# Two blocks of transformer in one kernel: the modulation vectors' pieces move from VectorE to ScalarE and GpSimd

## The reference

```
x = first_block(x, ...)         # 2 layers: dilated attention + FFN, gated linear attention + FFN
# second_block: 2 layers, each with N_MOD = 9 modulation vectors of D = 1024
c_act = silu(c)                                         # (1, 1024)
mod = split(c_act @ w_ada[l] + b_ada[l], 9)             # w_ada[l]: 1024 x 9216
h = modulate(rms_norm_2(x, ffn1_norm[l]), mod[0], mod[1])
...
def swiglu(h, w_gate_up, w_down):
    g, u = split(h @ w_gate_up, 2)
    return (silu(g) * u) @ w_down
```

## Time and profile before

| | |
|---|---|
| time, median of 3 runs | 3469.39 us (3467.5 to 3470.66) |
| profiled execution: its time and its span | 3467.5 us and 3467.5 us |
| busy: PE, PEld (weight loads) | 3438.4 us (99%), 2906.9 us (84%) |
| busy: DVE, ACT, POOL | 2446.7 us (71%), 1515.5 us (44%), 187.7 us (5%) |
| chain of work that ended last, by engine | PE 94%, DVE 3%, issue 1%, ACT 1% |
| DMA | 444.89 MB, mean 128 GB/s |

### The profile page before, as it was taken

How to read it: one execution, slowest core, us unless ns; L and a number is a source line. 1 busy time by engine, 2 the same in 40 slices (tenths; PEclk the granted TensorE clock), 3 DMA queues, 4 the chain that set the end, 5 groups by cost and what they waited for, 6 DMA issues and landing times.

```text
span 3467.5 us, 51118 instructions
## 1 busy us (share of the span) xinstructions
PE 3438.4 (99%) x19728; PEld 2906.9 (84%) x19728; DVE 2446.7 (71%) x4223; ACT 1515.5 (44%) x2603; POOL 187.7 (5%) x266
## 2 busy tenths in 40 slices
PE   9999999999999999999999999999999999999999
PEld 7777777888876788888999888899989998878998
DVE  5777775777766577777667767766686667677666
ACT  5555554322343332234444444444454444444444
POOL 0000000000000000000110000010001100000100
PEclk9999999999999999999999999999999999999999
DMA  4222223667421267744655322465446543225654
GB/s 148 80 73 77 80 65 104 223 220 227 129 72 55 73 223 219 226 156 116 152 143 144 86 73 79 128 150 145 126 133 152 147 122 89 68 69 154 152 145 108
DMA packets 207827, 444.89 MB, mean 128 GB/s; under 512 B 28976, under 2 KB 78512, under 8 KB 207600
## 3 DMA queue, kind: packets, MB, share of 16 engines
q1 hardware_dynamic: 171952, 325.55, 30.5%
q0 software_dynamic: 35648, 116.28, 14.2%
HBM read 438.73 MB, written 2.10 MB: 127 GB/s over the span
## 4 chain that ended last, share of the span: by engine, by line
PE 94%; DVE 3%; issue 1%; ACT 1%; DMA 0%; SPq 0%; DVEq 0%; ACTq 0%
PE psP L1423 18%; PE psP L1428 18%; PE psP L1424 18%; PE psS L1572 7%; PE psS L1573 7%; PE psS L1571 7%; PE psP L1653 3%; PE psP L1660 3%; PE psP L1654 3%; PE psS L1996 1%; PE psS L1716 1%; PE psM L2019 1%; PE psS L1880 1%; PE psS L1685 1%; PE psS L1698 0%
## 5 line engine op out<-in xcount | busy, mean ns | idle before, releaser
L1423 PE MATMUL psP<-a_hi,w_hi 128*128 128x512 f32 x1736 | 686.7, 396 | 1.2 <-ACT a_hi L1376 1.2
L1428 PE MATMUL psP<-a_lo,w_hi 128*128 128x512 f32 x1736 | 677.6, 392 | 0.0
L1424 PE MATMUL psP<-a_hi,w_lo 128*128 128x512 f32 x1736 | 676.8, 390 | 0.0
L819 ACT ACTIVATE w_hi<-raw 128x1024 fp32r<-128x1024 f32 (+3 forms) x411 | 341.4, 831 | 398.5 <-PE psP L1428 398.5
L2112 DVE TENSOR_TENSOR w_lo<-raw,w_hi 128x1024 fp32r<-128x1024 f32 (+3 forms) x411 | 386.7, 941 | 164.0 <-ACT w_hi L819 160.7
L1423 PE MATMUL psP<-h_hi,w_hi 128*128 128x512 f32 x1024 | 407.2, 398 | 4.1 <-ACT h_hi L911 2.3
L1424 PE MATMUL psP<-h_hi,w_lo 128*128 128x512 f32 x1024 | 399.4, 390 | 0.0
L1423 PEld LDWEIGHTS psP<-a_hi,w_hi 128*128 128x128 f32 x1736 | 326.8, 188 | 79.2 <-issue 15.8
L1428 PE MATMUL psP<-h_lo,w_hi 128*128 128x512 f32 x1024 | 391.8, 391 | 0.0
L2503 DVE TENSOR_TENSOR s_lo<-s_raw,s_hi 128x1024 fp32r<-128x1024 f32 (+1 forms) x288 | 314.5, 1092 | 104.8 <-ACT s_hi L982 104.7
L1428 PEld LDWEIGHTS psP<-a_lo,w_hi 128*128 128x128 f32 x1736 | 325.7, 188 | 71.2 <-DVE a_lo L3169 0.9
(11 more groups left out here) (412 smaller groups left out, 6146.8 us busy)
## 6 DMA issues: line engine op xcount, KB each, us to landing
s_raw<-in_gu SPq DMA_DIRECT2D x360, 256.0 KB, 3.5
adaw<-in_ada POOLq DMA_DIRECT2D x96, 768.0 KB, 5.4
raw<-in_gu SPq DMA_DIRECT2D x120, 512.0 KB, 3.7
s_raw<-in_gu POOLq DMA_DIRECT2D x144, 256.0 KB, 4.1
raw<-in_down SPq DMA_DIRECT2D x128, 256.0 KB, 2.9
raw<-in_qkv SPq DMA_DIRECT2D x40, 512.0 KB, 3.5
raw<-in_mix_in SPq DMA_DIRECT2D x34, 512.0 KB, 3.5
raw<-in_qkv SPq DMA_DIRECT2D x64, 256.0 KB, 3.0
```

What stands on the lines that cost most here:

```text
L819: nc.scalar.activation(w_hi[:, s, 0:cols], raw[:, s, 0:cols], copy).then_inc(hi_done, 1)
L1423: nc.tensor.matmul(psP[:, s, :], hi, rhs[0](kt), start=(n == 0), stop=False)
L1424: nc.tensor.matmul(psP[:, s, :], lo, rhs[0](kt), start=False, stop=False)
L1428: mm = nc.tensor.matmul(psP[:, s, :], w_hi[:, s, kt * P:kt * P + P], rhs[1](kt), start=False, stop=(n == K - 1))
```

## The change

A piece is now treated by two engines. ScalarE multiplies it by its column of cact: for kt = 0 into ada_acc, and for kt = 1 to 7 in place, in adaw. GpSimd then adds adaw to ada_acc, seven additions in each group. The slots are the same 60, now on ScalarE (ada_scale), always right behind hi. VectorE keeps only the folding, in the tenth slot of a group where it had the ninth. GpSimd issues the load of piece c + 4 behind the addition of piece c (for kt = 0, behind its scaling).

```
@@ GpSimd
+            def ada_load(c):
+                if c >= ADA_RING:
+                    old = c - ADA_RING
+                    if old % KT == 0:
+                        pool.wait_ge(ada_scaled, old + 1)
+                    else:
+                        pool.wait_ge(*ada_added.at(added_before(old) + 1))
+                pool.dma_start(adaw[:, c % ADA_RING, :], A["ada"][c]).then_inc(ada_landed[c % ADA_RING], 16)
+            def ada_add(c):
+                group, kt = divmod(c, KT)
+                pool.wait_ge(ada_scaled, c + 1)
+                if kt:
+                    total = ada_acc[:, group % 2, :]
+                    pool.wait_ge(*ada_added.at(added_before(c)))
+                    nc.gpsimd.tensor_tensor(total, total, adaw[:, c % ADA_RING, :], ALU.add).then_inc(ada_added.sem, 1)
             for F in (F0, F1):
                 pool.wait_ge(F.norm.acc_ready, F.norm.turns(0) + 1)
-                for c in range(F.ada * 48, F.ada * 48 + 48):
-                    pool.wait_ge(ada_used, c + 1)
-                    pool.dma_start(adaw[:, c % ADA_RING, :], A["ada"][c]).then_inc(ada_landed[c % ADA_RING], 16)
+                first_piece = F.ada * 48
+                for c in range(first_piece, first_piece + ADA_RING):
+                    ada_load(c)
+                for c in range(first_piece, first_piece + 48):
+                    ada_add(c)
+                    if c + ADA_RING < first_piece + 48:
+                        ada_load(c + ADA_RING)
@@ ScalarE, ffn
+                def ada_scale(count):
+                    for _ in range(count):
+                        group, kt = next(slices)
+                        if kt >= KT:
+                            continue
+                        c = group * KT + kt
+                        w, to = adaw[:, c % ADA_RING, :], ada_acc[:, group % 2, :]
+                        act.wait_ge(ada_landed[c % ADA_RING], (c // ADA_RING + 1) * 16)
+                        if kt == 0 and group >= 2:
+                            act.wait_ge(ada_folded, group - 1)
+                        nc.scalar.activation(w if kt else to, w, copy, scale=cact[:, kt:kt + 1]).then_inc(ada_scaled, 1)
                         hi(3, shapes[2 * j + 3])
+                        ada_scale(1)
                         pos.step()
...
                         hi(3, shapes[2 * j + 4])
+                        ada_scale(ADA_PER_PAIR - 1)
                         pos.step()
...
                         hi(3, shapes[2 * nf + m + 3])
+                        if not last:
+                            ada_scale(ADA_PER_DOWN)
                         pos.step()
@@ VectorE, folded
-                dve.wait_ge(ada_used, ADA_RING + (g + 1) * KT)
+                dve.wait_ge(*ada_added.at((g + 1) * (KT - 1)))
@@ VectorE, ffn
-                    dve.wait_ge(ada_landed[c % ADA_RING], (c // ADA_RING + 1) * 16)
-                    dve.wait_ge(ada_used, c + ADA_RING)
-                    if kt == 0:
-                        i = v.tensor_scalar(total, w, at, None, ALU.mult)
-                    else:
-                        i = v.scalar_tensor_tensor(total, w, at, total, ALU.mult, ALU.add)
-                    i.then_inc(ada_used, 1)
...
-                        if kt < KT:
-                            ada(group * KT + kt)
-                        elif kt == KT:
+                        if kt == KT + 1:
                             folded(group)
```

More of the change, by code:

```diff
@@ L528, in program @@
         cact_ready = sem("cact_ready")
-        ada_used = sem("ada_used")
+        ada_scaled = sem("ada_scaled")
         ada_folded = sem("ada_folded")
@@ L565, in program @@
         root_copied, ffn_silu, ffn_high = (Later(z, TOKEN_TILES - 8) for z in (probT1_ready, hlog_ready, hrstd_ready))
+        ada_added = Later(rot_ready, TOKEN_TILES - 8)
         ffn_rooted, r_silu = Later(hvar_ready, TOKEN_TILES - 8), Later(exp1_done, TOKEN_TILES - 8)
@@ L784, in _, with added_before @@
                 pool.dma_start(xT[:, p, :], A["x"][:, p, :]).then_inc(x_back[p], 16)
+            def added_before(c):
+                return c - c // KT - 1
+            def ada_load(c):
[13 more added lines that the diff above has]
+                    nc.gpsimd.tensor_tensor(total, total, adaw[:, c % ADA_RING, :], ALU.add).then_inc(ada_added.sem, 1)
             for F in (F0, F1):
                 pool.wait_ge(F.norm.acc_ready, F.norm.turns(0) + 1)
-                for c in range(F.ada * 48, F.ada * 48 + 48):
-                    pool.wait_ge(ada_used, c + 1)
-                    pool.dma_start(adaw[:, c % ADA_RING, :], A["ada"][c]).then_inc(ada_landed[c % ADA_RING], 16)
+                first_piece = F.ada * 48
[5 more added lines that the diff above has]
+                        ada_load(c + ADA_RING)
             def weight_sums(F, l):
@@ L921, in ffn @@
                 root_copy(F.norm, ffn_root)
+                first_group = 2 * len(PARTS) * F.ada
+                slices = iter([(group, kt) for group in range(first_group, first_group + 2 * len(PARTS)) for kt in range(KT + 2)])
+                def ada_scale(count):
[9 more added lines that the diff above has]
+                        nc.scalar.activation(w if kt else to, w, copy, scale=cact[:, kt:kt + 1]).then_inc(ada_scaled, 1)
                 for n, (f0, nf) in enumerate(PARTS):
@@ L945, in ffn @@
                             stream_square(m, N)
+                assert next(slices, None) is None
                 if g:
@@ L2353, in ffn @@
             def ffn(F, N, g, after_first):
-                def ada(c):
-                    group, kt = divmod(c, KT)
-                    w, total, at = adaw[:, c % ADA_RING, :], ada_acc[:, group % 2, :], cact[:, kt:kt + 1]
-                    dve.wait_ge(ada_landed[c % ADA_RING], (c // ADA_RING + 1) * 16)
-                    dve.wait_ge(ada_used, c + ADA_RING)
-                    if kt == 0:
-                        i = v.tensor_scalar(total, w, at, None, ALU.mult)
-                    else:
-                        i = v.scalar_tensor_tensor(total, w, at, total, ALU.mult, ALU.add)
-                    i.then_inc(ada_used, 1)
                 first_group = 2 * len(PARTS) * F.ada
@@ L2610, in _ @@
             v.memset(credit[:, 2:3], 0.0).then_inc(gmix_ready, 1)
-            v.memset(credit[:, 3:4], 0.0).then_inc(ada_used, ADA_RING)
             for k, started in enumerate((mix_ready, F0.a_ready, F1.a_ready, F2.a_ready, F3.a_ready, o1_ready)):
```

## The result

The changed kernel takes 3491.43 us (median of 4 runs, 3489.89 to 3491.73) against 3470.02 us for the kernel before: slower by a ratio of 1.0063, 95% interval 1.0052 to 1.0075, 21.4 us. The forecast was 3468.5 us. Its profiled execution spans 3488.6 us, 21.1 more than before.

The account below looks back on a forecast made before the run. TensorE bounds the kernel, busy 3438.4 of 3467.5 us. VectorE's relief 0, folding -0.9, ScalarE 0 and GpSimd 0 give a span of 3466.6 us, forecast as a 3468.5 us median; own range 3466 to 3471, 8-of-10 range 3465.5 to 3477.

Parts of the forecast that it names:

- The scaling: ScalarE in the feed-forward stages: 96 scalings of 1.55 us, 74 us a stage, always behind w_hi, cost 0.
- an addition: GpSimd: 84 additions, bounded between 1.81 and 5.43 us each, taken as 3.6 us, cost 0.
- ScalarE never waits for a piece: Piece loads in the feed-forward stages: landing has four slots or 21.4 us, leaving 15.5 us for the addition and its queue.
- GpSimd keeps up: GpSimd's group of pieces: 16.9 to 42.3 us of work in 53.5 us; behind only at 7.04 us an addition.
- rival B: Exclusion between VectorE and GpSimd overfills GpSimd's group from 4.3 us an addition; 3541 us at 5.43 us; chance 10%.
- The folding's 0.9 us: Last pair of each feed-forward stage: h_lo ahead of the folding saves 0.43 us, twice; gain 0.9 us.
- The expected share of ScalarE: Feed-forward stages: ScalarE near 50% busy, with 74 us of scalings a stage added to 85.8 of 317 us.
- that of VectorE: Feed-forward stages: VectorE's busy share some 25 points lower, from 75% to about 50%.
- the part on VectorE's margins: Gate and up halves: at most one addition each, holding VectorE at most 5.43 us, so the steady state holds.
- a margin of 7.3 us: Gate half: w_lo is done at 639.6 us and its weights are used at 646.94; the up half has the same.
- Rival A: Part ends only: additions block VectorE instructions with two SBUF inputs, delaying h_lo; 2.2 us in two stages, 3470.7 us; chance 10%.

Follow-up runs that it names:

- e7: Kernel before, with VectorE folding a group in its tenth slot instead of its ninth: 3467.66 against 3468.30 us, ratio 0.9997.
- e1: Changed kernel without GpSimd's 84 additions, all 96 scalings kept: 3468.05 us, ratio 0.9997.
- e3: Changed kernel with the multiplication prod taking the root from PSUM instead of SBUF: 3466.96 us, ratio 0.9994.
- e11: Changed kernel with each addition split into two of 768 columns, all arithmetic kept: 3471.42 us, ratio 1.0006.
- e5: Changed kernel with both scalings of a pair in the gate half, none in the up half: 3514.35 us, ratio 1.0134.
- e4: Changed kernel with each addition covering 768 of the 1536 columns, the other half left out: 3467.34 us, ratio 0.9996.
- e8: Changed kernel with a memset of ada_acc over 1536 columns in place of each addition: 3469.49 us (one run).

## Why the prediction was wrong

**Right.** The scaling costs 1.565 us (1.55 forecast), an addition 3.51 us (3.6 taken). The estimate from the Trainium skill's 4497 ns for 2048 columns (GPSIMD Engine Reference, section 3.1, Elementwise) was 3.4 us; the trace has 4% more. ScalarE never waits for a piece, GpSimd keeps up with gaps between the additions, and rival B's threshold of 4.3 us was not reached. The folding's 0.9 us is there (e7, and in the changed kernel's third parts, where TensorE has no gap). The expected share of ScalarE came, 154.9 of 317 us; that of VectorE did not, it was busy for 197.7 of 317 us (62%) where 25 points less than 75% were forecast, and the difference is in the instructions that were held.

**Wrong.** The step that failed is in the part on VectorE's margins: "A half pair holds at most one addition, and that can hold VectorE up by at most its own length, 5.43 us at the high end, so the steady state holds even if the two engines exclude each other". Two things in it are false.
First, the gate half meets two additions. That of the up half is scaled late, runs into the next gate half and holds w_lo; that of the gate half waits behind it on GpSimd and starts as w_lo ends, right on prod. Together 4.7 us.
Second, a margin of 7.3 us against TensorE is a stock, and I used it as if each pair brought it anew. What a pair brings anew is 10.88 us less its own loop, and I never added that up. The loop is 7.7 us (e1), so there are 3.15 us a pair for holds, and 4.7 us exceed them by 1.6. The stock is gone after a few pairs. The trace of before was enough to see it: the pair from 615.21 to 625.27 us ran at VectorE's own pace of 10.06 us with two pieces of 1.81 us in it, which leaves a bare loop of at least 6.4 us. So a pair had at most 4.4 us to spare, less than the one addition of 5.43 us that I allowed in each of its halves.

**Rival A had the mechanism and missed its size.** It held exclusion to matter at the part ends alone, once, for 1.1 us a stage, with an addition of 5.43 us. e1, e3 and the lengths of the held instructions show exclusion. It came in pair after pair where VectorE was behind, and collected at three part ends. The chance of 20% for A and B together was too low as well, for a price that no row showed. The Trainium skill's rule (SBUF — State Buffer, section Who interferes with whom) states that the two take turns for whole instructions. The trace agrees: prod takes 3.98 us against 0.68, with an addition of 3.55. I weighed the rule only against GpSimd's capacity (rival B), not against VectorE's loop.

**Not foreseen at all** was the stretch at the lower clock behind each stall. The terms are 15.2 us for the three stalls (4.3, 4.3 and 6.5), 1.0 for small ones in F1's second part and 7.4 for the clock, less 0.9 for the folding: 22.7 us. The starts of the last matmul differ by 20.4 us and the spans by 21.1; the 2.3 us between are the remainder that I have not traced.

## What to carry to other kernels

When work moves to GpSimd, list VectorE's instructions with two SBUF inputs beside it (here a TENSOR_SCALAR with one input was held too), and sum VectorE's loop with each of them longer by the rest of a GpSimd instruction. Compare that with the tempo of the engine that bounds; a margin that is only a stock doesn't count. If the sum is too long, one operand moved to PSUM (e3) or shorter GpSimd instructions (e11) give more than another slot (e5). And taking 164 us from an engine that isn't waited for gave nothing here, even without the damage (e1: 3468.05 against 3468.92 us).

## What the runs showed of the hardware that was not expected

- A VectorE instruction with one input can be held too. In the changed kernel, in the last down tile of F1's first part, the second of these two:

```profile
1369.24 0.42 DVE L2362 CAST turns<-posn 128x512 f32<-128x512 int32 x1
1369.70 3.64 DVE L2363 TENSOR_SCALAR ang<-turns,par 128x512 f32<-128x512 f32 x1
```

An addition runs beside it from 1369.56 us for 3.49 us; in the kernel before that TENSOR_SCALAR takes 0.49 us. It is part of the work behind which F1's second part starts late. The same instruction takes 1.98 us in e4, with an addition of half the columns, and 1.57 us in e8, where GpSimd only writes.
- The turns go both ways. In the changed kernel an addition recorded as beginning 0.38 us after a prod takes 3.67 us in place of 3.51, and one recorded 0.41 us after a w_lo (751.33 against 750.92 us) takes 4.17 us.
- In e5, w_lo's record begins at 624.43, 0.41 us ahead of the addition's at 624.84, and yet the addition ran first; so it was in all 24 such meetings of that run. In the changed kernel w_lo had the same lead twice (at 750.92 and 1386.22 us) and ran first both times. So the recorded starts don't tell which of the two goes first. What decides it was not tried.
